# A layer's feed-forward: rows turned as they stand, the norm's reciprocal root applied behind the up product and in the residual

## The reference, cut to what matters

```python
def rmsnorm(x, g):
    y = x * rsqrt(mean(x * x, axis=-1, keepdims=True) + EPS)
    return y * g

def swiglu(x, w_gate, w_up, w_down):
    return (silu(x @ w_gate) * (x @ w_up)) @ w_down

def second_block(x, ...):
    for l in range(2):
        x = x + 0.5 * swiglu(rmsnorm(x, ffn1_norm[l]), ffn1_w_gate[l], ffn1_w_up[l], ffn1_w_down[l])
        h = rmsnorm(x, mix_norm[l])
        ...                                   # attention branches, merged into y
        x = x + y @ w_out[l]
        x = x + 0.5 * swiglu(rmsnorm(x, ffn2_norm[l]), ffn2_w_gate[l], ffn2_w_up[l], ffn2_w_down[l])
    return rmsnorm(x, final_norm)
```

## Time and profile before

| | before |
|---|---|
| median of 3 runs | 2436.75 us (2433.3 to 2437.85) |
| the profiled execution | 2434.63 us, span 2432.9 us |
| TensorE busy | 2358.4 us, 97% of the span |
| VectorE busy | 1522.6 us, 63% |
| ScalarE busy | 1120.3 us, 46% |
| mean granted TensorE clock | 0.992 of full |
| HBM | 164 GB/s over the span |

### The profile page before, as it was taken

The page is one execution under the profiler, slowest core; times in us unless marked ns, Lnnn a source line. Parts: engine busy times, 40 slices in busy tenths (PEclk is TensorE's granted clock), DMA queues, the critical chain, the costliest instruction groups (busy, mean ns, idle before and its releaser), DMA issues.

```text
span 2432.9 us, 32937 instructions
## 1 busy us (share of the span) xinstructions
PE 2358.4 (97%) x13390; PEld 1985.3 (82%) x13390; DVE 1522.6 (63%) x2182; ACT 1120.3 (46%) x1687; POOL 13.1 (1%) x43
## 2 busy tenths in 40 slices
PE   7999999999999999999899999999999999999998
PEld 4877888888888888888788888888888888787887
DVE  4785233746747586666666568666666665776665
ACT  4221232525543335444544467554454455764444
POOL 0000000000000000000000000000000000000000
PEclk9999999999999999999999999999999999999999
DMA  7773222313431124455555554445545556344553
GB/s 303 275 291 139 87 90 100 139 53 139 156 138 70 70 94 159 173 190 190 193 189 190 204 181 155 139 166 190 189 167 190 192 183 225 139 148 158 189 192 137
DMA packets 57910, 399.64 MB, mean 164 GB/s; under 512 B 7785, under 2 KB 8305, under 8 KB 10272
## 3 DMA queue, kind: packets, MB, share of 16 engines
q1 hardware_dynamic: 52704, 383.80, 43.4%
q10 hardware_dynamic: 4264, 10.07, 1.2%
q0 software_dynamic: 800, 3.73, 0.5%
HBM read 396.52 MB, written 2.63 MB: 164 GB/s over the span
## 4 chain that ended last, share of the span: by engine, by line
PE 89%; DVE 4%; ACT 3%; DMA 2%; issue 1%; SPq 0%; DVEq 0%; ACTq 0%
PE pair L494 84%; DMA ring<-in_stream 2%; PE pair L828 1%; DVE ring_parts L2124 1%; PE pair L606 1%; PE pair L811 1%; PE pair L964 1%; PE pair L623 1%; ACT mix_high L1459 0%; ACT arena L1799 0%; ACT arena L1409 0%; ACT xT L1437 0%; PE pair L775 0%; PE pair L1242 0%; DVE rows L2221 0%
## 5 line engine op out<-in xcount | busy, mean ns | idle before, releaser
L494 PE MATMUL pair<-xT_parts,ring_high 128*128 128x512 f32 x2112 | 747.2, 396 | 3.7 <-DVE xT_parts L2106 3.7
L494 PE MATMUL pair<-xT_parts,ring_parts 128*128 128x256 f32 (+2 forms) x2448 | 694.0, 298 | 3.7 <-DVE ring_parts L2124 1.8
L2114 DVE TENSOR_TENSOR ring_parts<-ring,ring_high 128x2048 fp32r<-128x2048 f32 x198 | 453.5, 2292 | 152.0 <-ACT ring_high L1446 151.9
L494 PEld LDWEIGHTS pair<-xT_parts,ring_parts 128*128 128x128 f32 (+1 forms) x2448 | 461.2, 188 | 44.7 <-issue 9.6
L494 PEld LDWEIGHTS pair<-xT_parts,ring_high 128*128 128x128 f32 x2112 | 385.4, 188 | 80.0 <-issue 4.5
L1446 ACT ACTIVATE ring_high<-ring 128x2048 fp32r<-128x2048 f32 x198 | 378.3, 1911 | 143.3 <-DMA ring<-in_stream 143.2
L2124 DVE TENSOR_TENSOR ring_parts<-ring,mix_high 128x1024 fp32r<-128x1024 f32 x144 | 168.3, 1220 | 77.4 <-ACT mix_high L1459 77.0
L1491 ACT ACTIVATE arena<-pair 128x512 f32<-128x512 f32 x110 | 65.7, 597 | 310.2 <-PE pair L494 310.2
L1459 ACT ACTIVATE mix_high<-ring 128x1024 fp32r<-128x1024 f32 x144 | 143.0, 1049 | 100.5 <-DMA ring<-in_stream 96.8
L494 PE MATMUL pair<-ring_parts,xT_parts 128*128 128x512 f32 (+1 forms) x448 | 175.7, 392 | 2.1 <-ACT arena L1775 1.9
L494 PE MATMUL pair<-ring_parts,g_high 128*128 128x512 f32 x440 | 171.5, 390 | 0.0
(11 more groups left out here) (403 smaller groups left out, 3704.2 us busy)
## 6 DMA issues: line engine op xcount, KB each, us to landing
ring<-in_stream SPq DMA_DIRECT2D x338, 1024.0 KB, 4.8
xn<-in_mods SPq DMA_DIRECT2D x14, 1024.0 KB, 5.0
arena<-in_mods SPq DMA_DIRECT2D x14, 1024.0 KB, 5.7
arena<-in_bT ACTq DMA_DIRECT2D x1, 1536.0 KB, 8.7
bias_scratch<-bias_row POOLq DMA_DIRECT2D x1, 1536.0 KB, 8.0
X<-in_x ACTq DMA_DIRECT2D x1, 1024.0 KB, 11.9
X<-in_ctx ACTq DMA_DIRECT2D x1, 1024.0 KB, 16.4
arena<-in_bT ACTq DMA_DIRECT2D x1, 1024.0 KB, 7.5
```

The source lines that it names most:

```text
L494: m = pe.matmul(o, l, r, start=start, stop=stop)
L2114: dve.tensor_tensor(out=ring_r[:, slot].rearrange("p a b -> p (a b)"), in0=w, in1=high[:, slot, :], op=ALU.subtract).then_inc(low_ready, 1)
```

## The change

The four feed-forwards of the layers no longer wait for the norm's reciprocal root. `norm_late` turns the rows of X as they stand, by 16 plain transposes into PSUM (`late_bank`, two feature groups to a bank). ScalarE multiplies each group (128x256) by the gain straight into the high part, and VectorE does one `scalar_tensor_tensor` per group that multiplies the same PSUM by the gain and subtracts the high part. Three of ScalarE's four squares stay ahead of that, the last comes behind, and so do both roots, reciprocals and diagonals. The first up tile waits for one group at a time.

After the first up tile TensorE multiplies a tile of ones with the two diagonals (`rstd_sums`), which gives a 128x256 tile whose every row holds the reciprocal roots of the tokens. ScalarE copies it (`rstd_rows`), and VectorE multiplies the gate half of every up tile by it (`gate_scaled`) ahead of silu. The up half stays unscaled. The same factor is made good in the residual: `halved` multiplies by the column `half_rstd` in place of 0.5. The norms of the first block, of the mixers and of the end stay as they are.

```diff
--- before.py
+++ after.py
@@ -163,6 +163,8 @@
         ones = sb("ones", [P, S])
+        half_rstd = sb("half_rstd", [P, 2])
+        rstd_rows = room(6144, S)
         summing = ones[:, 0:64].rearrange("p (r c) -> p r c", c=32)
@@ -306,6 +308,9 @@
         resid = sem("residual_updated")
+        rstd_full = sem("rstd_rows_summed")
+        rstd_out = sem("rstd_rows_kept")
+        scaled = sem("gate_inputs_scaled")
         squares = sem("squares_of_half_summed")
...
@@ -454,6 +459,15 @@
             return order + [("down", FT // 2 - 2), ("down", FT // 2 - 1)]
+
+        def late_bank(k, upper):
+
+            at = ((4, 6), (5, 7) if upper else (2, 3))[k // 4][k % 2]
+            return bank[at][:, k % 4 // 2 * S:(k % 4 // 2 + 1) * S]
+
+        def rstd_bank(upper):
+
+            return bank[4 if upper else 5][:, 0:S]
@@ -628,7 +642,33 @@
-            def ffn(nt):
+            def norm_late(ready, upper):
+
+                for h in range(2):
+                    ready(h, 0)
+                    for t_ in range(2):
+                        if t_:
+                            ready(h, 1)
+                        for k in range(4 * h, 4 * h + 4):
+                            m = pe.transpose(late_bank(k, upper)[:, t_ * P:(t_ + 1) * P], X[:, t_, k * P:(k + 1) * P],
+                                             ident[:, :])
+                            if owed and k % 4 == 0:
+                                m.then_inc(owed.pop(), 1)
+                        m.then_inc(x_turned, 1)
+                c.rstd += 2
+                c.split += KD
+
+            def rstd_sums(upper):
+
+                for t_ in range(2):
+                    pe.wait_ge(rstd_done, c.rstd + t_ - 1)
+                    m = pe.matmul(rstd_bank(upper)[:, t_ * P:(t_ + 1) * P], ones[:, 0:P], diag[:, t_, :], start=True,
+                                  stop=True)
+                    if owed and t_ == 0:
+                        m.then_inc(owed.pop(), 1)
+                m.then_inc(rstd_full, 1)
+
+            def ffn(nt, late=None):
                 block_chunk.append(c.chunk)
@@ -650,10 +690,12 @@
                     for half, ks in steps:
-                        if f == 0 and half == 0:
+                        if f == 0 and half == 0 and late is None:
                             pe.wait_ge(x_split, c.split - (KD - max(ks.stop, 2) if nt == 4 else 2 - ks.start // 2))
...
                         for k in ks:
+                            if f == 0 and half == 0 and late is not None:
+                                pe.wait_ge(x_split, c.split - KD + k + 1)
                             wl, wh = weights(j, 2 * k + half, P)
@@ -698,6 +740,8 @@
                         beside_up(i)
+                    if late is not None and j == 0:
+                        rstd_sums(late)
                 c.chunk += BLOCK
@@ -1277,8 +1321,14 @@
                     bias_toeplitz()
-                norm()
-                ffn(2)
+                kept = 24 if c.layer else 16
+
+                def sums_ready(h, t_):
+                    pe.wait_ge(resid, kept + (2 * h + 2 if c.layer else 3 + h))
+
+                upper = c.layer == 0
+                norm_late(sums_ready, upper)
+                ffn(2, upper)
                 mix_chunk.append(c.chunk)
@@ -1331,8 +1381,13 @@
                 quad((yT_halves, yT_low), {(0, 2): sums_settled, (0, 3): lambda: flips(y2, 1, y_done, c.y)})
-                norm()
-                ffn(2)
+
+                def projected_ready(h, t_):
+                    m = c.acc - 4 + 2 * h + t_
+                    pe.wait_ge(evac[m % 4], m // 4 + 1)
+
+                norm_late(projected_ready, True)
+                ffn(2, True)
...
@@ -1439,6 +1495,38 @@
+            def norm_late(source, gain, upper, by_tile=False):
+
+                def halves(qs):
+                    for q in qs:
+                        t_, n = divmod(q, 2) if by_tile else divmod(q, 2)[::-1]
+                        if source == "residual":
+                            act.wait_ge(resid, c.resid - 4 + q + 1)
+                        else:
+                            m = c.acc - 4 + q
+                            act.wait_ge(evac[m % 4], m // 4 + 1)
+                        c.squares += 1
+                        act.activation(junk[:, q, :], X[:, t_, n * N:(n + 1) * N], ACT.Square, scale=D ** -0.5,
+                                       accum_out=ss[:, n, t_:t_ + 1]).then_inc(squares, 1)
+
+                halves(range(3))
+                for k in range(KD):
+                    if k % 4 == 0:
+                        act.wait_ge(x_turned, c.turned + 2 + k // 2)
+                    if k % 4 >= 2:
+                        act.wait_ge(x_split, c.split + k - 1)
+                    act.activation(xT_r[:, k, 0:S], late_bank(k, upper), ACT.Identity,
+                                   scale=gain[:, k:k + 1]).then_inc(x_whole, 1)
+                c.turned += 4
+                c.split += KD
+                halves(range(3, 4))
+                for t_ in range(2):
+                    c.sd += 1
+                    act.wait_ge(var_done, c.sd)
+                    act.wait_ge(squares, c.squares - (1 - t_ if not by_tile else 2 - 2 * t_))
+                    act.activation(sd[:, t_:t_ + 1], ss[:, 1, t_:t_ + 1], ACT.Sqrt,
+                                   bias=var[:, t_:t_ + 1]).then_inc(sd_done, 1)
+
             def split(b, j):
@@ -1467,7 +1555,7 @@
-            def ffn(nt, then_ffn=False, then_mix=None):
+            def ffn(nt, then_ffn=False, then_mix=None, late=None):
@@ -1492,7 +1580,11 @@
-                    act.wait_ge(both_done, c.f + f + 1)
+                    if late is None:
+                        act.wait_ge(both_done, c.f + f + 1)
+                    else:
+                        c.late += 1
+                        act.wait_ge(scaled, c.late)
                     if f >= 2:
@@ -1524,6 +1616,9 @@
                         cross_copy(i)
+                        if late is not None and i == 0:
+                            act.wait_ge(rstd_full, c.late // FT + 1)
+                            act.activation(rstd_rows, rstd_bank(late), ACT.Copy).then_inc(rstd_out, 1)
                         gate(i)
@@ -1891,9 +1986,9 @@
             def layer(l):
-                norm(2, "residual", lambda t_: gains2[:, 3 * l, :], lambda t_: None, by_tile=l == 0)
+                norm_late("residual", gains2[:, 3 * l, :], l == 0, by_tile=l == 0)
                 c.layer += 1
-                ffn(2, then_mix=l)
+                ffn(2, then_mix=l, late=l == 0)
                 norm(2, "residual", lambda t_: gains2[:, 3 * l + 1, :], lambda t_: None)
@@ -1963,8 +2058,8 @@
                 split(c.block, 1)
-                norm(2, "products", lambda t_: gains2[:, 3 * l + 2, :], lambda t_: None)
-                ffn(2, l == 0)
+                norm_late("products", gains2[:, 3 * l + 2, :], True)
+                ffn(2, l == 0, late=True)
@@ -2106,6 +2201,20 @@
+            def norm_late(gain, upper, ahead=None):
+
+                for k in range(KD):
+                    dve.wait_ge(x_whole, c.turned + k + 1)
+                    dve.scalar_tensor_tensor(out=xT_r[:, k, S:2 * S], in0=late_bank(k, upper), scalar=gain[:, k:k + 1],
+                                             in1=xT_r[:, k, 0:S], op0=ALU.mult, op1=ALU.subtract).then_inc(x_split, 1)
+                c.turned += KD
+                for t_ in rstds(2):
+                    dve.tensor_scalar(diag[:, t_, :], ident[:, :], rstd[:, t_:t_ + 1], None,
+                                      ALU.mult).then_inc(rstd_done, 1)
+                step(dve.tensor_scalar(half_rstd[:, :], rstd[:, 0:2], 0.5, None, ALU.mult))
+                if ahead:
+                    ahead()
+
             def low(b, j):
@@ -2134,7 +2243,7 @@
-            def ffn(nt, update, then_ffn=False, then_mix=None):
+            def ffn(nt, update, then_ffn=False, then_mix=None, late=False):
@@ -2168,6 +2277,15 @@
                                       op=ALU.add).then_inc(both_done, 1)
+
+                def gate_scaled(f):
+
+                    if f == 0:
+                        c.late += 1
+                        dve.wait_ge(rstd_out, c.late)
+                    dve.wait_ge(both_done, c.f + f + 1)
+                    dve.tensor_tensor(out=both[:, f % 2, 0, :], in0=both[:, f % 2, 0, :], in1=rstd_rows,
+                                      op=ALU.mult).then_inc(scaled, 1)
@@ -2197,6 +2315,8 @@
                         both_sum(i)
+                        if late:
+                            gate_scaled(i)
                         product(i)
@@ -2584,7 +2704,7 @@
                 cols = slice(n * N, (n + 1) * N)
-                dve.scalar_tensor_tensor(out=X[:, t_, cols], in0=src, scalar=0.5, in1=X[:, t_, cols],
+                dve.scalar_tensor_tensor(out=X[:, t_, cols], in0=src, scalar=half_rstd[:, t_:t_ + 1], in1=X[:, t_, cols],
                                          op0=ALU.mult, op1=ALU.add).then_inc(resid, 1)
@@ -2766,9 +2886,9 @@
```

(11 more changed lines are left out.)

## The result

After the change the kernel takes 2423.72 us, the median of six runs (2421.78 to 2431.49), against 2437.3 us for the kernel before, six runs (2433.24 to 2438.16). The ratio is 0.9956, with a 95% interval of 0.994 to 0.9972. That is 0.44% faster, and the whole interval lies beyond the 0.2% that a measurement of this kernel can tell. The medians lie further apart, 13.6 us, than the 10.7 us of the ratio, and the interval reaches from 6.8 to 14.6 us: the times alone give the gain to some 4 us. The forecast was 2426.3, in a range of 2422.0 to 2432.5.

A forecast was written before the change was run, and what follows sets the result against it. TensorE, busy for 97% of the span, bounds the kernel. Gains of 2.97 + 2.97 + 2.41 + 2.24 - 0.2 = 10.4 us take the profiled 2434.63 to 2424.2; forecast median 2426.3, range 2422 to 2432.5.

The forecast's parts named there:

- the four starts: Beginnings of the two feed-forwards in each of layers 0 and 1, where a 6.1 us gap was to shrink.
- The start in B and D: Second feed-forwards of layers 0 and 1: first up product 3.96 us earlier, at T + 2.14; each gains 2.97 us.
- T: End of TensorE's last product before a feed-forward's start; before the change the first up product came at T + 6.10.
- Pace: First up tile: products wait for column groups to be split by ScalarE and VectorE, giving back 0.40 us per start.
- The sums: TensorE's new `rstd_sums` after the first up tile: two fp32 products, four passes, giving back 0.59 us per start.
- `halved`: Residual step that now reads a column for its factor: 0.05 us more per feed-forward, 0.2 us in all.
- C: Layer 1's first feed-forward: second up tile waits 0.56 us for its split weights; gain 2.41 us, bounds 1.7 and 3.2.
- A: Layer 0's first feed-forward: turning at low clock, back no earlier than before, costing 0.35 us; gain 2.24, bounds 0.8 and 3.3.
- Edits costed at nothing: In the up tiles, 88 VectorE multiplies of `gate_scaled`, plus the rstd rows' copy and weight chunks: no time added.
- The clock rival: After 2.1 us without a real product TensorE's clock falls in B, C and D too: 2433.5 us, chance 0.08.
- The rival "slower": The added multiply makes VectorE the bound of up tiles: 2445 us and up, chance 0.05.
- Faster, same, slower: Chances for the whole kernel: 0.83 faster, 0.11 within 0.2% of no change, 0.06 slower.

The follow-up runs named there:

- the round with four multiplies: The changed kernel with three more unread multiplies, shaped like the gate multiply, on VectorE in each up tile; one run took 2429.76 us.

## Why the prediction was right, point by point

The direction, the mechanism and the size were right: at the four starts 10.6 us were forecast (10.4 with what `halved` costs) and 12.48 found, and the ratio of the runs gives 10.7. The forecast for the profiled execution was 2424.2, and it was 2421.78. That 10.7 lies so close to 10.4 is in part luck. Each of the four starts gained 0.4 to 0.6 us more than forecast, and a fall of the clock in the attention of layer 1, which the forecast doesn't have, took some 2 us back in the profiled execution.

- **The start in B and D** was given as T + 2.14 and came at T + 2.05 (D too). Root and diagonal are off the path, and they alone are 2.94 of the 3.44 us: shown by the run that puts them back with TensorE kept at work.
- **Pace.** Forecast 0.40. From the first up product to the sums are 5.96 us against some 5.66, so 0.30.
- **The sums** were the term furthest off: 0.59 forecast, 0.36 measured. I took 1.17 us for eight passes from the chain in the earlier trace rows, which holds the last pass's way to its result; passes follow each other every 0.109 us (the run with products). "At the transposes' rate it would be 0.2" was the bound from the other side, and the truth lies between. Leaving the sums out gave back 0.36 and 0.40.
- **`halved`**, 0.05 us per place, was right: it went from 0.69 to 0.75 us, and TensorE's pause ahead of the two mixers' norms behind it from 1.18 to 1.24.
- **C** was to wait 0.56 us for the split of tile 1's weights, and waited 0.36; the place was right. C gained 3.05, 2.41 forecast. That ScalarE took its first group at T + 0.91 and not T + 0.98 is part of that.
- **A** gained 2.65, 2.24 forecast, inside its bounds; tile 1 waited 0.27 us for the split weights (0.63 from the sums' start to tile 1, less 0.36), where 0.5 was forecast. Moved by the 3.05 us by which this execution came to it earlier, the forecast has the turning at 1157.65 (it was 1157.72), the clock back at 1161.95 (about 1162.6) and tile 1 at 1168.40 (1168.04). The stretches of the kernel after:

```profile
1154.00:1157.70 3.70, 0.00 (x0) 0.00 (x0) 3.33 (x9) 2.76 (x11) 0.00 (x0) 0.74 0.01 2
1157.70:1161.39 3.69, 3.67 (x17) 3.67 (x18) 1.78 (x5) 2.20 (x6) 0.00 (x0) 0.50 0.51 169
1162.00:1163.00 1.00, 1.00 (x6) 0.86 (x5) 0.92 (x3) 0.79 (x3) 0.00 (x0) 0.70 0.43 180
1163.00:1164.00 1.00, 1.00 (x8) 0.87 (x7) 0.88 (x2) 1.00 (x5) 0.00 (x0) 1.00 0.00 0
```

The low clock covers all the turning and the first up products, as forecast. It came back 0.65 us later against the work than "no earlier than before". The rule of the Trainium skill (TensorE: Matmul & The Clock Gate, Part 4: PE-mode transpose) would have had A about 1 us later than forecast; A was 0.36 earlier. Products in place of the transposes brought the clock back no sooner, 5.1 us after their start. How the low clock falls in A is chance, though, and so are some tenths of its gain: its spell began 2.1 us into TensorE's pause in this profile and 4.7 us after the pause's start in the second one of the same kernel, where tile 1 came 0.55 us earlier.

- **Edits costed at nothing** did cost nothing: 177.56 us behind tile 1 in B with the 88 multiplies, 177.50 without them.
- **The clock rival** named a real hazard and the wrong trigger. In this kernel the granted clock is 1.00 at B, C and D. It fell there when TensorE was idle for 2.7 us in one piece, as with the root put back, and not with transposes in the pause, so turning by transposes was not the danger. The idle time after the change is 0.3 us. The argument against the rival looked at the 6.1 us gaps of the earlier trace rows alone, where the idle time is in two pieces of 1.18 and 0.72 us; the kernel before has a pause of 2.2 us elsewhere that did bring the clock down (the last section shows it).
- **The rival "slower"** had its threshold too low. It was to decide from 0.8 us per multiply more than 0.46, and with 1.1 more the steady part still had a microsecond to spare. The mistake was to count VectorE's waits in a down tile as work.
- **Faster, same, slower** stood at 0.83, 0.11 and 0.06, and the interval of the ratio lies in the first.

## What to carry to other kernels

When a normalisation is linear in what follows, take its root off the path by applying it to the result; here the 6.1 us ahead of the first product became 2.05 (at tile 1 in B the gain is 3.44 us, since the sums and the slower pace take a part of it) for 88 small multiplies on an engine that had the time, and the gain is the number of such starts times what the queue of the first engine loses to the wait. Cost each engine's slack over a whole round of the schedule, and sort its waits: a round trip to another engine stays when the engine gets later (1.08 us of each 6.66 here), a wait for work that is not yet due vanishes (1.26 in the down tile). By busy time alone the round with four multiplies would have had 3.2 us to spare; it had 1.02. And look at the places where the round is broken (three up tiles in a row). A duration from a chain of waits holds one latency; to price an instruction in a queue, take the distance between starts.

## What the runs showed of the hardware

- A pause of 2.7 us on TensorE brought 3.4 us at 1.2 GHz, at three of three starts, and cost 0.8 us each; 24 transposes in the pause avoided it at three of three. Shorter pauses did it too. In the norm of the first block's last feed-forward, which the change doesn't touch, TensorE is idle for 2.2 us in one piece, and in all ten profiles the clock fell for 3.4 us, 0.4 to 1.4 us after it had started again. Behind another pause, of 1.9 us (429.54 to 431.45 before), it fell in six of the ten. The pause of 2.2 us in the kernel before, and the low clock behind it:

```profile
964.34:966.54 2.20, 0.00 (x0) 0.00 (x1) 2.08 (x6) 1.43 (x4) 0.15 (x1) 1.00 0.01 4
967.04:970.45 3.41, 3.41 (x18) 3.41 (x18) 1.09 (x4) 2.20 (x7) 1.08 (x3) 0.50 0.59 207
```

- Sixteen products of 128x128 in fp32 take 3.48 us from start to next product, 32 passes of 0.109; sixteen transposes 1.66. One product of 256 columns took 0.24 us where two of 128 took 0.36: the wider one is cheaper by a third.
- In the attention of layer 1 the clock fell for a spell, far from the change. The chain of waits of the kernel after there:

```profile
2041.90 1.18 issue
2043.07 0.69 PE pair L1249 x4
...
2046.56 2.58 PE pair L508 x10
```

and the stretch in it:

```profile
2044.00:2046.00 2.00, 2.00 (x18) 1.92 (x14) 1.02 (x1) 0.00 (x0) 0.00 (x0) 0.50 0.89 373
```

The section from 2043.07 to 2046.56 takes 3.5 us; the same section took 1.9 before (2054.60 to 2056.53). The pause ahead of it, 1.18 us, is the same in both. The fall is in eight of the nine profiles with the change, of its variants too, for 3.4 to 10.2 us, and not in the run with products nor in the one profile of before. Whether the change brings it about or one profile of before happened to miss it isn't settled: no run here moved it by design. What it costs shows in the stretch from the last product of C's feed-forward to the last one ahead of D: 253.3 us before and 253.5 with products, without a fall; 255.1 to 255.9 with one of 3.4 us; 256.8 and 257.6 with 6.8; 259.0 with 10.2. So it is worth 2 us or more, which the change would gain on top if it could be avoided.
